# A RWKV-7 scan whose 64-row operands are stacked into 128-row ones

## What is computed

```
def _wkv7_step(S, inp):
    r_t, w_t, k_t, v_t, aa_t, bb_t = inp
    sa = jnp.einsum('zbhij,zbhj->zbhi', S, aa_t)
    S = S * w_t[..., None, :] + sa[..., :, None] * bb_t[..., None, :] + v_t[..., :, None] * k_t[..., None, :]
    y = jnp.einsum('zbhij,zbhj->zbhi', S, r_t)
    return S, y
```

## Time and profile before

| | us |
|---|---|
| median of three runs | 4858.02 (4856.51 to 4867.45) |
| the profiled execution | 4869.98 |
| its span | 4867.9 |
| TensorE busy in the span | 4311.4 (89%), 50312 matmul passes |
| VectorE, ScalarE, GpSimd busy | 1928.2, 1292.7, 1279.7 |

### The profile page before, as it was taken

The page is one execution under the profiler, slowest core; times in us unless marked ns, Lnnn a source line. Parts: engine busy times, 40 slices in busy tenths (PEclk is TensorE's granted clock), DMA queues, the critical chain, the costliest instruction groups (busy, mean ns, idle before and its releaser), DMA issues. The chain is left out here.

```text
span 4867.9 us, 112762 instructions
## 1 busy us (share of the span) xinstructions
PE 4311.4 (89%) x50312; PEld 3614.9 (74%) x50312; DVE 1928.2 (40%) x3380; ACT 1292.7 (27%) x2542; POOL 1279.7 (26%) x794
## 2 busy tenths in 40 slices
PE   3899898999999996996958888888878999999997
PEld 2688856888888885885847777777755888888886
DVE  3011054154252443226146666666633244242441
ACT  1111065211011112236124444444422211011110
POOL 2111032311111115111125454555512311111110
PEclk8899999999999997998979999999989999999998
DMA  3211242311313112121232222221222311313214
GB/s 130 65 59 55 69 134 73 119 39 53 107 40 105 56 58 80 69 78 43 85 89 67 67 68 72 63 74 56 63 100 87 126 35 50 111 40 100 65 50 161
DMA packets 402639, 372.41 MB, mean 77 GB/s; under 512 B 63057, under 2 KB 370513, under 8 KB 399985
## 3 DMA queue, kind: packets, MB, share of 16 engines
q1 hardware_dynamic: 390320, 354.75, 23.6%
q10 hardware_dynamic: 11840, 10.49, 0.6%
HBM read 257.68 MB, written 107.48 MB: 75 GB/s over the span
## 5 line engine op out<-in xcount | busy, mean ns | idle before, releaser
L422 POOL TENSOR_TENSOR f_wlow<-f_raw,f_whigh 128x1024 fp32r<-128x1024 f32 (+1 forms) x152 | 360.1, 2369 | 1671.2 <-ACT f_whigh L493 1671.2
L478 PE MATMUL f_ps<-fx_hh,f_whigh 128*128 128x512 f32 (+1 forms) x2112 | 529.6, 359 | 0.0
L478 PE MATMUL f_ps<-fx_hl,f_whigh 128*128 128x512 f32 (+1 forms) x2112 | 528.5, 358 | 0.0
L478 PE MATMUL f_ps<-fx_hh,f_wlow 128*128 128x512 f32 (+1 forms) x2112 | 528.2, 358 | 0.0
L493 ACT ACTIVATE f_whigh<-f_raw 128x1024 fp32r<-128x1024 f32 (+1 forms) x152 | 156.6, 1030 | 922.7 <-PE f_ps L478 895.0
L478 PEld LDWEIGHTS f_ps<-fx_hl,f_whigh 128*128 128x128 f32 x2112 | 348.7, 189 | 65.8
L478 PEld LDWEIGHTS f_ps<-fx_hh,f_whigh 128*128 128x128 f32 x2112 | 348.5, 189 | 65.6
L478 PEld LDWEIGHTS f_ps<-fx_hh,f_wlow 128*128 128x128 f32 x2112 | 348.2, 188 | 65.7
L478 PE MATMUL f_ps<-mo_oh,f_whigh 128*128 128x512 f32 (+1 forms) x1440 | 360.8, 359 | 26.2 <-POOL f_wlow L422 26.2
L1605 PE MATMUL sc_inv_ps<-sc_tf,sc_bl 64*64 64x64 f32 x6400 | 283.0, 223 | 105.3 <-DVE sc_tf L1956 59.8
L478 PE MATMUL f_ps<-mo_ol,f_whigh 128*128 128x512 f32 (+1 forms) x1440 | 360.4, 359 | 0.0
(11 more groups left out here) (268 smaller groups left out, 8383.8 us busy)
## 6 DMA issues: line engine op xcount, KB each, us to landing
f_xo<-xres SPq DMA_DIRECT2D x64, 640.0 KB, 4.0
xres<-f_xo SPq DMA_DIRECT2D x56, 640.0 KB, 2.9
f_raw<-in_ffn_w_gate SPq DMA_DIRECT2D x44, 512.0 KB
f_raw<-in_ffn_w_up SPq DMA_DIRECT2D x44, 512.0 KB
sc_rk<-rkvl SPq DMA_DIRECT2D x80, 256.0 KB, 3.4
rkvl<-ri_ot SPq DMA_DIRECT2D x28, 640.0 KB, 2.9
f_raw<-in_ffn_w_down SPq DMA_DIRECT2D x32, 448.0 KB
qkv_raw<-in_na_w_qkv SPq DMA_DIRECT2D x24, 512.0 KB, 5.7
```

Of the source, the lines that this page charges most:

```text
L422: nc.gpsimd.tensor_tensor(wlow[:, m % 2, 0:kt], raw[:, 0:kt], whigh[:, m % 2, 0:kt].bitcast(F32), ALU.subtract).then_inc(cut_lo, 1)
L478: last = nc.tensor.matmul(ps[:, m % 2, n, 0:count], w[:, m % 2, k], x[:, k, t0:t0 + count], start=(k == 0 and w is whigh and x is xh), sto ...
```

## The change

Tokens and channels are stacked on the partition axis, so that one operand has 128 rows where there were two of 64. The new gx holds, per chunk and head, the query rows (0 to 63) above the Gram rows (64 to 127), each with its y counterpart beside it; sv holds, for each chunk and head, the state above v, and u above v; t0 holds turned b above turned k. So:

- gram and turn give 128 output partitions at once: weights on 64 rows and 128 columns, 8 matmuls a call for gram in place of 16, and 16 for turn in place of 24. The v of a turn is given 64 columns of other data ahead of it (vpad) so that it lands on partitions 64 to 127.
- x_product is 4 matmuls of 128 rows a step in place of 8 of 64 rows.
- u_product keeps 4 matmuls a step, which now all write partitions 0 to 63.
- s_product is 2 matmuls with the identity over 128 moving columns and 4 of 128 rows, in place of 12; all write partitions 0 to 63.
- y_products has for each chunk 4 matmuls of 64 rows and then 4 of 128 rows, in place of 12.
- ScalarE gets bm_copy (2 copies a call, 64x256), query_copy (2 copies, 64x512), read_copy (1 copy, 64x512), and in turn_copy two 64x512 copies of v in place of one 128x256. u_copy is 64x256 in place of 128x128.
- On VectorE gram_out loses bm and has two 512-column operations in place of 256, 256 and 512, and waits for bm_copy; state_out is 64x256 in place of 128x128; the decays pc are written by two operations in place of one. The store of y is two DMAs in place of three, with two buffers in place of three.

```diff
-        vb = ph.sb("vb", [P, 4, Z, W])
+        vpad = ph.sb("vb", [P, 4, C + Z * W])
+        vb = vpad[:, :, C:].rearrange("p r (z n) -> p r z n", z=Z)
...
-        pc = ph.sb("pc", [P, 4, Z, U])
+        pc = ph.sb("pc", [P, 4, Z, U, 2])
 
         rec = ph.sb("rec", [P, 4, Z, U, 4, C])
-        yt = ph.sb("yt", [P, 3, Z, W])
+        yt = ph.sb("yt", [P, 2, Z, W])
...
-        ga = ph.sb("ga", [P, 3, Z, U, C])
-        nr = ph.sb("nr", [P, 4, Z, 2, U, C])
+        gx = ph.sb("gx", [P, 4, Z, 2, U, 2, C])
+        rl = ph.sb("rl", [P, Z, U, C])
...
-        vt = ph.sb("vt", [P, 2, Z, U, C])
         xs = ph.sb("xs", [P, Z, C])
-        tu = ph.sb("tu", [P, 2 * U, Z, C])
-        st = ph.sb("st", [P, 2 * U, Z, C])
+        sv = ph.sb("sv", [P, 2, 2, Z, U, 2, C])
...
-        x_ps, u_ps, s_ps = (chain_ps[:, :, i * C:(i + 1) * C] for i in range(3))
+        x_ps, u_ps, s_ps = chain_ps[:, :, 0:C], chain_ps[0:HD, :, C:3 * C], chain_ps[0:HD, :, 4 * C:6 * C]
...
+        def slot(h, z):
+            return h if z == 0 else 1 - h
+
         def side(h, z):
-            return halves[h] if z == 0 else halves[1 - h]
+            return halves[slot(h, z)]
...
-                    c = col_of(0, j)
-                    sp.dma_start(ysc[:, p, 0, c:c + W], yt[:, G % 3, 0]).then_inc(y_stored[G % 3], 16)
-                    c = col_of(1, j)
-                    for h, rows in enumerate(halves):
-                        sp.dma_start(ysc[rows, p, 1, c:c + W], yt[side(h, 1), G % 3, 1]).then_inc(y_stored[G % 3], 16)
+                    for z in range(Z):
+                        c = col_of(z, j)
+                        sp.dma_start(ysc[:, p, z, c:c + W], yt[:, G % 2, z]).then_inc(y_stored[G % 2], 16)
...
-                    for s in range(U):
-                        u = unit(z, s)
-                        for a in range(2):
-                            for rows in halves:
-                                last = nc.tensor.matmul(gram_ps[rows, a, s * 128:(s + 1) * 128], rec[rows, r, z, u, a],
-                                                        rec[rows, r, z, u, 2:4].rearrange("p a n -> p (a n)"), start=True, stop=True)
+                    for u in range(U):
+                        for h, rows in enumerate(halves):
+                            last = nc.tensor.matmul(gram_ps[:, slot(h, z), u * 128:(u + 1) * 128], rec[rows, r, z, u, 0:2].rearrange("p a n -> p (a n)"),
+                                                    rec[rows, r, z, u, 2:4].rearrange("p a n -> p (a n)"), start=True, stop=True)
...
-                    for s in range(U):
-                        u = unit(z, s)
-                        for a in range(2):
-                            for rows in halves:
-                                nc.tensor.matmul(turn_ps[z][rows, 0, a * W + s * C:a * W + (s + 1) * C], rec[rows, r, z, u, a], ident[rows, rows],
-                                                 start=True, stop=True)
-                        for rows in halves:
-                            last = nc.tensor.matmul(turn_ps[z][rows, 1, s * C:(s + 1) * C], vb[rows, r, z, u * C:(u + 1) * C], ident[rows, rows],
-                                                    start=True, stop=True)
+                    for u in range(U):
+                        for h, rows in enumerate(halves):
+                            nc.tensor.matmul(turn_ps[z][:, slot(h, z), u * C:(u + 1) * C], rec[rows, r, z, u, 0:2].rearrange("p a n -> p (a n)"),
+                                          ident[rows, rows], start=True, stop=True)
+                        for h, rows in enumerate(halves):
+                            at = z * W + u * C
+                            last = nc.tensor.matmul(turn_ps[z][:, slot(h, z), W + u * C:W + (u + 1) * C], vpad[rows, r, at:at + 2 * C], ident[rows, rows], start=True, stop=True)
...
+                        pe.wait_ge(a_al, G + 1)
                     for z in range(Z):
-                        for h, rows in enumerate(halves):
-                            nc.tensor.matmul(x_ps[side(h, z), z], ga[rows, G % 3, z, s], vt[rows, G % 2, z, s], start=True, stop=False)
-                    for z in range(Z):
-                        for h, rows in enumerate(halves):
-                            last = nc.tensor.matmul(x_ps[side(h, z), z], rec[rows, G % 4, z, unit(z, s), 2], st[rows, (4 * G + s) % (2 * U), z],
-                                                    start=False, stop=True)
+                        u = unit(z, s)
+                        for h in range(2):
+                            last = nc.tensor.matmul(x_ps[side(h, z), z], gx[:, G % 4, z, slot(h, z), u, 0], sv[:, G % 2, 0, z, u, slot(h, z)],
+                                                    start=True, stop=True)
...
-                            last = nc.tensor.matmul(u_ps[rows, z], rf[side(h, z), G % 3, z, s], xs[side(h, z), z], start=True, stop=True)
+                            q = slot(h, z)
+                            last = nc.tensor.matmul(u_ps[:, q, z * C:(z + 1) * C], rf[halves[q], G % 3, z, unit(z, s)], xs[halves[q], z],
+                                                    start=True, stop=True)
...
-                        for rows in halves:
-                            nc.tensor.matmul(s_ps[rows, z], ident[rows, rows], st[rows, g, z], start=True, stop=False)
-                    for z in range(Z):
-                        for rows in halves:
-                            nc.tensor.matmul(s_ps[rows, z], t0[rows, G % 2, z, 1, s], vt[rows, G % 2, z, s], start=False, stop=False)
-                    for z in range(Z):
-                        for rows in halves:
-                            last = nc.tensor.matmul(s_ps[rows, z], t0[rows, G % 2, z, 0, s], tu[rows, g, z], start=False, stop=True)
+                        nc.tensor.matmul(s_ps[:, z], ident[0:HD, 0:HD], sv[0:HD, G % 2, 0, z, unit(z, s)].rearrange("p q n -> p (q n)"),
+                                         start=True, stop=False)
+                    for q in range(2):
+                        for z in range(Z):
+                            u = unit(z, s)
+                            last = nc.tensor.matmul(s_ps[:, z, q * C:(q + 1) * C], t0[:, G % 2, z, q, u], sv[:, G % 2, 1, z, u, q],
+                                                    start=False, stop=q == 1)
...
+                    pe.wait_ge(a_rl, G + 1)
...
-                    for s in range(U):
-                        g = (4 * G + s) % (2 * U)
-                        to = [slice(unit(z, s) * C, (unit(z, s) + 1) * C) for z in range(Z)]
-                        for h, rows in enumerate(halves):
-                            for z in range(Z):
-                                nc.tensor.matmul(y_ps[side(h, z), z, to[z]], st[rows, g, z], rec[rows, G % 4, z, unit(z, s), 3], start=True, stop=False)
-                        for h, rows in enumerate(halves):
-                            for z in range(Z):
-                                nc.tensor.matmul(y_ps[side(h, z), z, to[z]], tu[rows, g, z], nr[rows, G % 4, z, 0, s], start=False, stop=False)
-                        for h, rows in enumerate(halves):
-                            for z in range(Z):
-                                last = nc.tensor.matmul(y_ps[side(h, z), z, to[z]], vt[rows, G % 2, z, s], nr[rows, G % 4, z, 1, s], start=False, stop=True)
+                    for u in range(U):
+                        to = slice(u * C, (u + 1) * C)
+                        for z in range(Z):
+                            for h, rows in enumerate(halves):
+                                r = rl[0:HD, z, u] if h else rec[0:HD, G % 4, z, u, 3]
+                                nc.tensor.matmul(y_ps[rows, z, to], sv[0:HD, G % 2, 0, z, u, slot(h, z)], r, start=True, stop=False)
+                        for z in range(Z):
+                            for h, rows in enumerate(halves):
+                                q = slot(h, z)
+                                last = nc.tensor.matmul(y_ps[rows, z, to], sv[:, G % 2, 1, z, u, q], gx[:, G % 4, z, q, u, 1], start=False, stop=True)
...
-                    nc.scalar.activation(t0[:, G % 2, z].rearrange("p a s n -> p (a s n)"), turn_ps[z][:, 0], ACT.Copy)
-                    nc.scalar.activation(vt[:, G % 2, z].rearrange("p s n -> p (s n)"), turn_ps[z][:, 1, 0:W], ACT.Copy).then_inc(a_turn[z], 1)
+                    nc.scalar.activation(t0[:, G % 2, z].rearrange("p q u n -> p q (u n)"), turn_ps[z][:, :, 0:W], ACT.Copy)
+                    v = turn_ps[z][HD:P, :, W:2 * W].rearrange("p q (u n) -> p q u n", n=C)
+                    nc.scalar.activation(sv[HD:P, G % 2, 0, z].rearrange("p u q n -> p q u n"), v, ACT.Copy)
+                    nc.scalar.activation(sv[HD:P, G % 2, 1, z].rearrange("p u q n -> p q u n"), v, ACT.Copy).then_inc(a_turn[z], 1)
+
+                def bm_copy(G, z):
+                    act.wait_ge(pe_gram[z], G + 1)
+                    if G >= 1:
+                        act.wait_ge(g_bl[z], G)
+                    for h, rows in enumerate(halves):
```

(58 more changed lines are left out.)

29 lines of the change are left out of this document (16 added, 13 removed).

## The result

The changed kernel takes 4940.52 us (median of four runs, 4931.90 to 4966.58), the kernel before 4860.77 in the same comparison: a ratio of 1.0172, 95% interval 1.0132 to 1.0212. The forecast was +96 us, measured were +80. The profiled execution took 4931.90 us, with a span of 4929.9; it is the fastest of the four, 62 us above the profiled one of before. Of the variant y_sixteen_blocks one execution, 5243.65 us, counts as slow, and the times given for that kernel are those of the other three.

What follows compares the result with a forecast made beforehand. It took TensorE's in-order list as the bound, with a ring of ScalarE and VectorE answers late at few places. Terms summed to +2.8 us a group, +2.4 after the walk, times 40 +96: 4954 us, range 4845 to 5025.

Steps and rivals of the forecast that it cites:

- occupancy: Array time of TensorE's passes in the changed blocks, from gram's -1.7 to s_product's +0.8: +0.6 us a group.
- changes of form: TensorE empties where passes of different form meet, such as 64*64 and 128*64: 23 at 0.15, +3.5 us a group.
- the stand before inverse(3): gram_out starts only after bm_copy, lengthening TensorE's stand at s = 0: +0.5 us a group; query_copy adds nothing.
- issue waits: TensorE's waits for a late instruction stream, 2.6 us a group, follow the pass count: -0.6, bounds 0 and -1.2.
- Rival (a): 64*64 and 128*64 passes follow each other without emptying the array: +1.1 us a group, 4902 us; chance 0.14.
- The absorbed 1.2: Some added TensorE time falls where it already stands, in 1.7 us of inverse waits: -1.2 us a group.
- Rival (d): The number of instructions is the bound: -6 us a group, about 4618 us; chance 0.01.
- Rival (b): Turn's weight loads hide, form changes are cheap, issue waits shrink by 1.2: -1.0 us a group, 4818 us; chance 0.15.
- Rival (c): ScalarE's queue sets the pace, delaying copies TensorE waits for: +5.1 us a group, 5062 us, half 5010; chance 0.07.
- the walk through a group: Step-by-step pricing of one group: the stand before inverse(7) at s = 2 takes 0.4, leaving +2.4 us.

Runs made afterwards that it cites:

- y_sixteen_blocks: Changed kernel with the two forms of y_products alternating per direction too, 16 blocks in place of 8: 5180.13 us, 1.065 times the kernel before.
- strict_early: Changed kernel with gram_out's first operation starting when gram ends, only the second waiting for bm_copy: 4917.31 us.
- y_snake: Changed kernel with every second chunk of y_products doing its 128-row products first, 4 changes of form a group less: 4942.04 us.
- turn_single: Changed kernel with the turns issued as transposes, one pass each in place of two: 4942.98 us.
- three_edits: Changed kernel with the edits of strict_early, y_snake and turn_single, and query_copy moved to s = 1: 4822.65 us, 0.9899 of the kernel before.

## Why the prediction was right, and where not

The table is in us a group. The measured column comes from the distances between the start of one pass and the start of the next, sorted by what lies between them: nothing, a change of form, or a wait. It is taken over the groups at full clock among groups 3 to 36, which last 26.7 us before (32 groups) and 27.6 after (27 groups).

| term | forecast | measured |
|---|---|---|
| occupancy | +0.6 | -0.1 (gram -1.6, turn +0.7, x -0.1, u +0.2, s +0.5, y +0.3, inverse -0.2) |
| changes of form | +3.5 | +4.0 (24 more outside waits, 0.15 us each after passes of 64 columns, 0.20 after 128) |
| waits for other engines | +0.5 for the stand before inverse(3), -1.2 absorbed | +0.8 (3.2 to 4.0; of it idle time 2.1 to 2.6) |
| issue waits | -0.6 | -3.8: all of them |
| low clock | not in the sum | +0.3 |

A price of 0.15 for a change and one for each pass share a distance at their border, so the first two rows are best taken together: +4.1 forecast, +3.9 measured.

- **Occupancy** and changes together held. Column halves run side by side (x_product's 8 passes start in pairs, 59 ns from pair to pair), and so do row halves (gram's 16, in pairs 112 ns apart). The passes of s_product follow at 0.065 us in place of 0.058, and turn's pairs at 0.11, near the 0.107 of the earlier trace rows.
- **Changes of form** held, for the pair that was not in the trace too. A group of after has the 31 changes that were counted, and the experiments on y_products gave +1.2 for 8 more and -0.6 for 4 fewer. Rival (a) is out: the gaps are 0.15.
- **The stand** had the right size, but half its mechanism. The prediction wrote that query_copy "adds nothing unless both slip"; it held p_copy(2) as long as gram_out held level_out, and strict_early alone brought 0.2 of 0.7.
- **The absorbed 1.2** did not come. TensorE's idle time behind other engines is 2.1 us a group before and 2.6 after, 0.5 more, which is the stand: none of the added work fell into waits that were there.
- **The issue waits** are the step that failed most. I let them follow the count of passes and bounded them at -1.2; they went altogether. Their idle time was 2.7 us a group, and from start to start, with 0.24 us from the last pass's start to the idle time at each of some 4.6 waits, they took 3.8. The bound was drawn from proportion alone, with no row for it. Rival (d), a gain from the count as such, stays wrong: the stream of passes takes 19.0 us a group, and took 19.1. But part of what it spoke of is real, in that the waits at the borders of 256 records are gone: 118 of 206 borders had one in the steady part of before, and none of the 153 of after.
- **The clock** was not in the sum. It costs some 13 us in the scan of the profiled execution (39 groups that take 1089.8 us in place of 39 x 27.6), and it decides more than that in the variants.
- **Rival (b)** needed cheap changes or hidden loads; neither is there. **Rival (c)** did not come: TensorE's waits for ScalarE's copies are 0.4 us of 900, though strict_early shows that ScalarE was only just in time before inverse(3).

The sum for the span: 39 groups from the first x_product to the last group's, 1039.8 us before and 1089.8 after, +50. Filling the pipeline takes 7 us more and what follows the last group's start 5: +62, the difference of the profiled executions. The medians differ by 80; the other three executions of after, 8 to 35 us slower than the profiled one, have no trace here, so how the remaining 18 are made up stays open.

The terms of the table add up to +0.9 at full clock and +1.2 with the clock, where the forecast had +2.8, and +2.4 after the walk through a group (it looked for a group of some 29 us): 1.1 us a group too much at the walk's figure, some 45 us. Between the terms, the issue waits were 3.2 us too small; the other way go the waits for other engines with 1.5 and the clock with 0.3. In the total, the 12 us at the ends of the scan and the open 18 hide most of the 45. So the mechanism that makes the kernel slower was right, and that the forecast came within 16 us is partly luck: errors had opposite signs.

## What to carry to other kernels

Before stacking operands to fill more rows, list the forms of the matmuls in the order TensorE issues them and price each change at what neighbouring stages show (0.15 us here): here 24 more changes cost 4 us a group, while 176 passes fewer left the stream of passes as long as it was. Judge such a change by the length of a steady group at full clock and by the granted clock separately, because the clock gave back here what TensorE saved in y_snake (0.6 us a group at full clock, mean clock 0.95) and turn_single (1.2 us, 0.89), and the savings came out where the stands were shortened too, in three_edits (2.3 us, 1.00). And when an engine loses instructions, look first at whether its waits named "issue" can vanish as a whole, as the 90.9 us in 900 did here: hold their places against the transfers of its "instruction" queue, 256 records of TensorE each in these traces.

## What the runs showed of the hardware that I had not expected

- TensorE's granted clock fell in stretches of kernels that never left it idle there for more than 1.6 us: its mean is 0.80 in the steady part with 31 + 8 changes of form a group, 0.98 with 160 passes more, and the version with more work is 51 us faster.
- Less work took the same time: turn_single issues 32 passes fewer a group, is 1.2 us shorter at full clock, and takes 4942.98 us beside the 4940.52 of the changed kernel.
- Transposes with weights of 64 rows and 128 columns were not paced by the 0.107 us of the earlier trace rows. In turn_single the pairs follow at 0.063 us, where the two-pass products take 0.11:

```profile
3032.63 0.23 PE L1585 MATMUL sc_gram_ps<-sc_ident,sc_rec 64*128 64x64 f32 x2
3032.69 0.23 PE L1589 MATMUL sc_gram_ps<-sc_ident,sc_vb 64*128 64x64 f32 x2
3032.75 0.23 PE L1585 MATMUL sc_gram_ps<-sc_ident,sc_rec 64*128 64x64 f32 x2
```

- The issue waits of TensorE stand where one block of 256 records ends and the next begins, 118 of 120 in before, and 115 of them end 1.2 to 1.6 us after a transfer of 16 KB has landed on the queue named "instruction". They are not proportional to the instructions: 90.9 us in 900 at 29.0 passes a microsecond, 1.9 at 24.3.
